# Tokens loaded in quarters of columns, the transposed banks read by ScalarE alone, squares after the tiles, two idle products

## What is computed

```python
h = rms_norm(x, norm1)
z = h @ w_in                        # 2048 x 5120: u, q, f, i, g
pool_out = pool_mix(u)              # trailing means over 2/4/8/16 tokens, a linear map for each group
o = hgrn2_recurrence(q, f, i) ...   # 8 heads, 128 x 128 state, norm and gate
x = x + concat(pool_out, o) @ w_o
x = x + (silu(h2 @ w_gate) * (h2 @ w_up)) @ w_down     # h2 = rms_norm(x, norm2)
y = rms_norm(x, norm_f)
```

## Time and profile before

| | us |
|---|---|
| median of the runs | 1494.37 |
| lowest, highest | 1490.41, 1495.2 |
| span of the profiled execution (first to last instruction) | 1492.4 |
| PE busy | 1459.7 (98%) |
| DVE busy | 805.1 (54%) |
| ACT busy | 550.0 (37%) |
| POOL busy | 188.2 (13%) |

### The profile page before, as it was taken

One profiled execution on the slowest core, in us unless ns is written; L12 is line 12 of the kernel. 1 busy time (PEld: TensorE's weight loads), 2 busy tenths in 40 slices (PEclk: granted clock), 3 DMA queues, 4 the chain that ended last, 5 costly groups with the idle time before them and its releaser, 6 DMA issues.

```text
span 1492.4 us, 27027 instructions
## 1 busy us (share of the span) xinstructions
PE 1459.7 (98%) x9928; PEld 1439.3 (96%) x9928; DVE 805.1 (54%) x1200; ACT 550.0 (37%) x823; POOL 188.2 (13%) x202
## 2 busy tenths in 40 slices
PE   7999999999999999999999999999999999999996
PEld 5999999899999999999999999999999999999996
DVE  4656788877765554444444544444444444444443
ACT  6442443344443343333333333333333333333443
POOL 0253434333112210000000000000000000000131
PEclk9998999999999999999999999999999999999998
DMA  8444544444465555554565555565554556555453
GB/s 223 137 129 124 138 122 137 119 114 122 124 168 141 148 145 157 141 156 123 150 185 144 142 141 142 140 168 150 159 141 133 149 147 165 154 152 141 119 148 114
DMA packets 409519, 214.52 MB, mean 144 GB/s; under 512 B 4093, under 2 KB 407757, under 8 KB 409420
## 3 DMA queue, kind: packets, MB, share of 16 engines
q1 hardware_dynamic: 391207, 203.52, 50.1%
q10 hardware_dynamic: 18277, 10.52, 2.6%
HBM read 206.14 MB, written 7.89 MB: 143 GB/s over the span
## 4 chain that ended last, share of the span: by engine, by line
PE 83%; DVE 10%; issue 4%; ACT 2%; DMA 1%; DVEq 0%; ACTq 0%; SPq 0%
PE bank L366 26%; PE bank L367 26%; PE bank L368 26%; DVE qr L1193 2%; DVE w_lo L1016 2%; DVE t L1180 1%; ACT w_hi L685 1%; DVE sc L1208 1%; PE bank L512 1%; DMA xt<-in_x_sample 1%; PE bank L462 0%; DVE sn L1252 0%; DVE scs L1208 0%; PE bank L410 0%; PE bank L412 0%
## 5 line engine op out<-in xcount | busy, mean ns | idle before, releaser
L366 PE MATMUL bank<-a_hi,w_hi 128*128 128x320 f32 x2048 | 646.2, 316 | 0.0
L367 PE MATMUL bank<-a_lo,w_hi 128*128 128x320 f32 x2048 | 635.4, 310 | 0.0
L368 PE MATMUL bank<-a_hi,w_lo 128*128 128x320 f32 x2048 | 635.3, 310 | 0.0
L1016 DVE TENSOR_TENSOR w_lo<-w_raw,w_hi 128x1024 fp32r<-128x1024 f32 (+1 forms) x416 | 467.3, 1164 | 150.1 <-ACT w_hi L685 149.2
L685 ACT ACTIVATE w_hi<-w_raw 128x1024 fp32r<-128x1024 f32 (+1 forms) x416 | 387.4, 968 | 158.5 <-PE bank L368 148.3
L366 PEld LDWEIGHTS bank<-a_hi,w_hi 128*128 128x128 f32 x2048 | 386.9, 189 | 2.4
L367 PEld LDWEIGHTS bank<-a_lo,w_hi 128*128 128x128 f32 x2048 | 387.2, 189 | 0.7
L368 PEld LDWEIGHTS bank<-a_hi,w_lo 128*128 128x128 f32 x2048 | 386.8, 189 | 0.0
L366 PE MATMUL bank<-h_hi,w_hi 128*128 128x320 f32 x704 | 217.7, 309 | 0.0
L367 PE MATMUL bank<-h_lo,w_hi 128*128 128x320 f32 x704 | 216.5, 308 | 0.0
L368 PE MATMUL bank<-h_hi,w_lo 128*128 128x320 f32 x704 | 216.5, 308 | 0.0
(11 more groups left out here) (218 smaller groups left out, 1195.6 us busy)
## 6 DMA issues: line engine op xcount, KB each, us to landing
w_raw<-in_w_gate SPq DMA_DIRECT2D x44, 1024.0 KB, 5.6
w_raw<-in_w_up SPq DMA_DIRECT2D x44, 1024.0 KB, 5.6
w_raw<-in_w_down SPq DMA_DIRECT2D x64, 704.0 KB, 4.8
w_raw<-in_w_in SPq DMA_DIRECT2D x39, 1024.0 KB, 5.8
w_raw<-in_w_o SPq DMA_DIRECT2D x16, 1024.0 KB, 6.1
s<-in_state_hgrn ACTq DMA_DIRECT2D x8, 512.0 KB, 4.3
out<-sn ACTq DMA_DIRECT2D x8, 512.0 KB, 7.3
xt<-in_x_prompt SPq DMA_DIRECT2D x3, 512.0 KB, 9.2
```

The lines of the kernel that those rows point to most:

```text
L366: pe.matmul(out, whi[:, par_, cols], r_hi, start=(k == 0), stop=False)
L367: pe.matmul(out, whi[:, par_, cols], r_lo, start=False, stop=False)
L368: last = pe.matmul(out, wlo[:, par_, cols], r_hi, start=False, stop=(k == last_k))
L1016: dve.tensor_tensor(wlo[:, par_, cols], raw[:, par_, cols], whi[:, par_, cols].bitcast(F32), SUB)\
```

## The change

Tokens are loaded in four quarters of 512 columns, not in two halves of 1024. SyncE's order becomes: first and second quarter of the first prompt tile and the samples, the first 8 tiles of slab 0, then third and fourth quarter of all three token tiles. ScalarE's queue issues two quarters of the second prompt tile. TensorE waits for a quarter ahead of tiles 0, 4, 8 and 12.

ScalarE copies every transposed tile to `x_res`, and takes a_hi from the bank for odd tiles alone. VectorE no longer reads the banks: for even tiles it takes a_hi from `x_res` (a tensor_scalar), and a_lo of all tiles from `x_res`. Four banks are free for reuse by one count, `xres_act`. ScalarE's two pieces of slab 0 follow tiles 3 and 11 (1 and 8 before), VectorE's follow tiles 4 and 12 (3 and 9 before). The lower bound's maximum stands after slab 1.

All six squares stand on ScalarE after slab 1. TensorE does two products of the matrix of ones by 512 columns of ones into a bank that is not in use yet, one ahead of the identity's wait and one behind norm1's transpose.

```diff
--- before.py
+++ after.py
@@ -28,6 +28,7 @@
 D = 2048
 KD = D // P
 HD = D // 2
+QD = D // 4
 TP, NB, TS = 256, 8, 8
 NS = NB * TS
 HB, HS = NB // 2, NS // 2
@@ -199,14 +200,14 @@
         ident_loaded, masks_loaded, norm1_loaded, par_loaded, w0_loaded, wp_loaded, cache_loaded, s0_loaded = (
             sem(n) for n in ("ident_loaded", "masks_loaded", "norm1_loaded", "par_loaded", "w0_loaded", "wp_loaded",
                              "cache_loaded", "s0_loaded"))
-        x_loaded = [[sem(f"x_loaded{half}{i}") for i in range(3)] for half in range(2)]
+        x_loaded = [[sem(f"x_loaded{quarter}{i}") for i in range(3)] for quarter in range(4)]
         fill_done, par_t, par_ready, lb_max, lb_exp, lb_ready = (
             sem(n) for n in ("fill_done", "par_t", "par_ready", "lb_max", "lb_exp", "lb_ready"))
         dve_link, newton_step = sem("dve_link"), sem("newton_step")
         ss_ready, rms_std, rms_diag, rms_bcast, rms_ready, stat_mm = (
             sem(n) for n in ("ss_ready", "rms_std", "rms_diag", "rms_bcast", "rms_ready", "stat_mm"))
-        xt_t, xres_act, ahi_ready, alo_ready = (
-            sem(n) for n in ("xt_t", "xres_act", "ahi_ready", "alo_ready"))
+        xt_t, xres_act, ahi_act, ahi_dve, alo_ready = (
+            sem(n) for n in ("xt_t", "xres_act", "ahi_act", "ahi_dve", "alo_ready"))
         t_ones, tails_ready, sc_zero, acc_zero, pad_zero, cache_tr, cache_in, win_step, win_ready, fix_ready, pooled_ready = (
             sem(n) for n in ("t_ones", "tails_ready", "sc_zero", "acc_zero", "pad_zero", "cache_tr", "cache_in", "win_step", "win_ready", "fix_ready",
                              "pooled_ready"))
@@ -281,11 +282,11 @@
                     eng.dma_start(prow[at:at + rows, :], src).then_inc(signal, 16)
                 at += rows
 
-        def load_x(eng, half, i):
-
-            cols = slice(half * HD, (half + 1) * HD)
+        def load_x(eng, quarter, i):
+
+            cols = slice(quarter * QD, (quarter + 1) * QD)
             rows, src = (P, x_prompt[0, i * P:(i + 1) * P, cols]) if i < 2 else (NS, x_sample.rearrange("b t d -> (b t) d")[:, cols])
-            eng.dma_start(xt[0:rows, i, cols], src).then_inc(x_loaded[half][i], 16)
+            eng.dma_start(xt[0:rows, i, cols], src).then_inc(x_loaded[quarter][i], 16)
 
 
         @block.sync
@@ -301,11 +302,14 @@
             sp.dma_start(cst[:, C_ID:C_ID + P], consts[:, C_ID:C_ID + P]).then_inc(ident_loaded, 16)
             load_x(sp, 0, 0)
             load_x(sp, 0, 2)
+            load_x(sp, 1, 0)
+            load_x(sp, 1, 2)
             w0 = raw[:, 0, :].rearrange("p (k c) -> p k c", c=P)
             k_mid = HALF[0][1]
             sp.dma_start(w0[:, 0:k_mid, :], win_v[:, 0:k_mid, 0:P]).then_inc(w0_loaded, 16)
-            for i in range(3):
-                load_x(sp, 1, i)
+            for quarter in range(2, 4):
+                for i in range(3):
+                    load_x(sp, quarter, i)
             sp.dma_start(w0[:, k_mid:KD, :], win_v[:, k_mid:KD, 0:P]).then_inc(raw_loaded[0], 16)
             load_params(sp, PARAMS[1:], par_loaded)
             load(1, 1, win_v, (0, KD), P)
@@ -401,20 +405,29 @@
 
             def x_transposes(k):
 
-                if k % (KD // 2) == 0:
+                if k % (KD // 4) == 0:
                     for i in range(3):
-                        pe.wait_ge(x_loaded[k // (KD // 2)][i], 16)
+                        pe.wait_ge(x_loaded[k // (KD // 4)][i], 16)
                 b4 = (SA, SB, SC, TV)[k % 4]
                 if k >= 4:
-                    pe.wait_ge((xres_act, alo_ready)[k % 2], (k // 2 - 1, k - 3)[k % 2])
+                    pe.wait_ge(xres_act, k - 3)
                 pe.transpose(b4[:, 0:P], xt[:, 0, k * P:(k + 1) * P], ident)
                 pe.transpose(b4[:, P:TP], xt[:, 1, k * P:(k + 1) * P], ident)
                 pe.transpose(b4[:, TP:N], xt[0:NS, 2, k * P:(k + 1) * P], ident[0:NS, 0:NS]).then_inc(xt_t, 1)
 
 
+            def keep_busy(count):
+
+                for _ in range(count):
+                    pe.matmul(zb[1][:, :].rearrange("p (a b) -> p a b", b=P), ones[:, :],
+                              ones[:, :].unsqueeze(1).to_broadcast([P, 4, P]), start=True, stop=True)
+
+            pe.wait_ge(fill_done, 1)
+            keep_busy(1)
             pe.wait_ge(ident_loaded, 16)
             pe.wait_ge(norm1_loaded, 16)
             pe.transpose(TK[:, 0:KD], prow[0:KD, :], ident[0:KD, 0:KD]).then_inc(par_t, 1)
+            keep_busy(1)
             for k in range(AHEAD):
                 x_transposes(k)
 
@@ -425,7 +438,7 @@
                 if k == 2:
                     pe.wait_ge(par_loaded, 16 * (len(PARAMS) - 1))
                     pe.transpose(TK[:, P:P + n_par], prow, ident[0:n_par, 0:n_par]).then_inc(par_t, 1)
-                pe.wait_ge(ahi_ready, k + 1)
+                pe.wait_ge((ahi_dve, ahi_act)[k % 2], k // 2 + 1)
                 pe.wait_ge(alo_ready, k + 1)
 
             def rms_first():
@@ -687,37 +700,36 @@
 
             load_params(act, PARAMS[:1], norm1_loaded)
             load_x(act, 0, 1)
+            load_x(act, 1, 1)
 
             act.wait_ge(fill_done, 3)
             act.activation(warm[:, 0:1], epst[:, 0:1], ACT.Sqrt)
 
             def square(half, i):
                 rows, at = (P if i < 2 else NS), 2 * i + half
-                act.wait_ge(x_loaded[half][i], 16)
+                for quarter in range(2 * half, 2 * half + 2):
+                    act.wait_ge(x_loaded[quarter][i], 16)
                 after(act, ss_ready, 3 * half + i)
                 act.activation(junk[0:rows, :], xt[0:rows, i, half * HD:(half + 1) * HD], ACT.Square,
                                accum_out=stat[0:rows, at:at + 1]).then_inc(ss_ready, 1)
 
-            for i in range(2):
-                square(0, i)
             act.wait_ge(par_ready, 1)
             for k in range(KD):
                 act.wait_ge(xt_t, k + 1)
                 bk = (SA, SB, SC, TV)[k % 4]
-                act.activation(a_hi[:, k, :], bk[:, 0:N], ACT.Copy, scale=pcol("norm1", k)).then_inc(ahi_ready, 1)
-                if k % 2 == 0:
-                    act.activation(x1[:, k, :], bk[:, 0:N], ACT.Copy).then_inc(xres_act, 1)
-                if k == 1:
+                if k % 2 == 1:
+                    act.activation(a_hi[:, k, :], bk[:, 0:N], ACT.Copy, scale=pcol("norm1", k)).then_inc(ahi_act, 1)
+                act.activation(x1[:, k, :], bk[:, 0:N], ACT.Copy).then_inc(xres_act, 1)
+                if k == 3:
                     act.wait_ge(w0_loaded, 16)
                     hi_piece(0, 0, 0, HALF[0])
-                if k == 3:
-                    square(0, 2)
-                if k == 8:
+                if k == 11:
                     act.wait_ge(raw_loaded[0], 16)
                     hi_piece(0, 0, 1, HALF[1])
             split_hi(1, 1)
-            for i in range(3):
-                square(1, i)
+            for half in range(2):
+                for i in range(3):
+                    square(half, i)
             act.wait_ge(ss_ready, 7)
             act.activation(stat[:, 9:12], stat[:, 6:9], ACT.Sqrt, bias=epst[:, 0:1], scale=1.0 / D).then_inc(rms_std, 1)
 
@@ -1055,23 +1067,29 @@
                 link(dve.tensor_tensor(lbt[:, 4, :], lbt[:, 1, :], lbt[:, 0, :], MUL))
                 dve.tensor_scalar(lbt[:, 5, :], lbt[:, 4, :], -1.0, 1.0, MUL, ADD).then_inc(lb_ready, 1)
 
-            for k in range(KD):
-                bk = (SA, SB, SC, TV)[k % 4]
-                dve.wait_ge(ahi_ready, k + 1)
-                if k % 2 == 1:
-                    dve.tensor_copy(x1[:, k, :], bk[:, 0:N])
-                else:
-                    dve.wait_ge(xres_act, k // 2 + 1)
-                src = (x1[:, k, :], bk[:, 0:N])[k % 2]
-                dve.scalar_tensor_tensor(out=a_lo[:, k, :], in0=src, scalar=pcol("norm1", k),
+            def normed_hi(k):
+
+                dve.wait_ge(xres_act, k + 1)
+                dve.tensor_scalar(a_hi[:, k, :], x1[:, k, :], pcol("norm1", k), None, MUL).then_inc(ahi_dve, 1)
+
+            def normed_lo(k):
+                dve.wait_ge(xres_act, k + 1)
+                dve.wait_ge((ahi_dve, ahi_act)[k % 2], k // 2 + 1)
+                dve.scalar_tensor_tensor(out=a_lo[:, k, :], in0=x1[:, k, :], scalar=pcol("norm1", k),
                                          in1=a_hi[:, k, :].bitcast(F32), op0=MUL, op1=SUB).then_inc(alo_ready, 1)
-                if k == 3:
+
+            for k in range(0, KD, 2):
+                normed_hi(k)
+                if k:
+                    normed_lo(k - 1)
+                normed_lo(k)
+                if k == 4:
                     lo_piece(0, 0, 0, HALF[0])
-                if k == 9:
+                if k == 12:
                     lo_piece(0, 0, 1, HALF[1])
-                if k == 12:
-                    lower_bound_max()
+            normed_lo(KD - 1)
             split_lo(1, 1)
+            lower_bound_max()
             dve.wait_ge(ss_ready, 6)
```

## The result

| | before | after |
|---|---|---|
| median, us | 1494.37 (17 runs, 1486.14 to 1495.44) | 1499.53 (17 runs, 1496.43 to 1500.95) |
| ratio of after to before | | 1.0039, 95% interval 1.0028 to 1.0050 |
| profiled execution, its own time (span) | 1494.37 (1492.4) | 1498.68 (1496.6) |
| first transpose of tokens, us | 9.66 | 8.31 |
| first product, us | 17.86 | 17.63 |

The medians are 5.2 us apart, and the ratio is 0.39% over 1. The forecast was 1495.4, 1.0 us slower, with a range up to 1498.2; it had the sign right and missed the size, and the measured time lies over the range.

The account below looks back on a forecast made before the run. TensorE, busy 98% of the span, was taken to set the time. Start -2.7, split's order +1.3 and squares +2.4 summed to +1.0 us: 1495.4 us, range 1488.4 to 1498.2.

Parts of the forecast that it names:

- Transposes start at 6.9: At the start, the samples' first quarter lands at 6.8 (bounds 6.2 to 7.6), so transposes start 2.7 us sooner.
- The new wait for `w_lo`: Ahead of the ninth tile's transposes, TensorE idles from 14.2 to 15.5; first product at 16.4, leaving 1.4 us gained.
- the landing L: Landing of the samples' first token quarter, taken as 6.8 us; the w_lo piece is ready at L + 8.7.
- The squares follow the tiles: First norm: six squares on ScalarE after slab 1 make TensorE wait 2.4 us, until 42.0, for the norm's products.
- No slack behind 42 us: After the first norm nothing is changed and PE has no slack, so the 1.0 us loss stays.
- The clock falls in the wait: In the new wait before the norm's products the clock falls; +1.8 us, up to +5; chance 0.12.
- rival (b): Slower: the clock falls in the new wait before the norm's products; 1497.2, up to 1500.4 us; chance 0.12.
- (c): At the start, quarters land no sooner than 8 us since the queues interleave; +1.2 more, 1496.6 us; chance 0.08.
- The idle products: Ahead of the tokens, two products on ones end by 4.9 us, cost nothing and bring no clock gain.
- Rival (a): The clock stays up from the idle products on; -6.0 us at the norm, 1488.4 or 1490.3; chance 0.18.

Follow-up runs that it names:

- the run with the wait filled: Changed kernel with three idle products of 512 columns ahead of TensorE's wait for the norm's diagonals; 1495.03 us, ratio 1.0015.
- the dense start on the changed kernel: Changed kernel with three squares back in the loop, five idle products ahead of the tokens, eight short ones among transposes, one long ahead of unit 0; 1484.65 us.
- the early pieces: Changed kernel with slab 0's first pieces sooner, w_hi behind tile 1 and w_lo behind tile 2; 1499.28 us, ratio 1.0034.
- the run with everything together: Changed kernel with first quarter alone in the queues, slab 0's first pieces sooner, three squares in the loop, five idle products and eight short ones; 1488.01 us.

## Why the prediction was wrong, by its own steps

**Transposes start at 6.9: missed by 1.4 us.** Measured 8.31. The landing that I put at 6.8, and at 7.6 if ScalarE's second quarter ran level, was at 8.17: that case was the true one, and it cost 0.6 us more than its bound. The run with the first quarter alone in the queues landed at 6.7, where I had put the value for the undisturbed queue (6.8). The mistake was to take the undisturbed case although the change itself put a second transfer into ScalarE's queue. The lag in bytes from one place can't be carried to another when what follows in the queues is different.

**The new wait for `w_lo`: right.** 1.3 us predicted, 1.09 measured; the first product stands 9.6 us behind the landing L in my sum (8.7 + 0.92), 9.5 in the trace. With the true L the sum gives 17.8, and 17.63 was measured. The gain at the first product, 1.4 us forecast, was 0.2.

**The squares follow the tiles: right in mechanism, and short by what the start had lost.** ScalarE's last tile came at 30.59 (29.4 forecast), the squares were 1.265 us apart (1.235), and the norm's products at 43.29 (42.0). Take the late start of 1.2 us off, and 0.1 us is left.

**No slack behind 42 us: right.** The 2.3 to 2.4 us are still there 80 us later, at the pause (127.41 against 125.04).

**The clock falls in the wait: this is the step that failed.** The sum priced the new wait by its length alone and put the clock behind it at nothing; it stood only as rival (b), with a chance of 0.12 and a price of 1.8 us. It fell in three profiled runs with late squares (at 45.1, 43.1 and 41.6 us), where it cost 1.7, 2.9 and 3.2 us, and in each of them delay and clock add up to the longer span within 0.2 us. My reason against it was wrong too: I said that the wait had to grow past the 2.4 us of the sum. A wait of 1.95 us was enough, and the row that I cited myself had a pause of 1.99 us, shorter than the wait that I forecast. In the changed kernel's own profiled run a wait of 1.76 us had no fall behind it. For its other runs the fall is inferred: from their mean clocks, and from the run with the wait filled, where it fits a gain of some 2 us.

With the clock in the sum: 1.0 + 1.3 for the late start + 1.8 for the clock = 4.1, and 1498.5 with the 1494.4 of before, against 1499.5 measured. Some 1 us is open; the price of 1.8 was at the low end of the 1.7 to 3.2 us seen, and the profiled run, without the fall, stayed low for 3.4 us longer at 127.5 to 141.2 us. I also kept (b) and (c) apart, as if only one could come. (c), a first quarter that lands after 8 us, came with the landing at 8.17, and the range ended below the sum of the two.

**The idle products: right that they bring nothing; the reason is only half borne out.** No gain, and no cost that could be told: the clock was lost at 8.1, before the first product. I had named the idle time and the transposes as what would lose it. In the profiled run it fell in the idle time, ahead of the first transpose of tokens, and in the run with five idle products it outlasted 4.6 us of transposes and fell in the wait behind them. The Trainium skill, "TensorE: Matmul & The Clock Gate", Part 4, says that transposes in PE mode do not count as busy for the clock in the way products do. The traces agree in so far as the transposes of the kernel before, at the lower level from 9.66 us, did not raise it; that transposes lose a raised clock no run here shows.

**Rival (a): near in its price, for another kernel.** In the dense start on the changed kernel, with the clock held, the loop takes 1.06 us a tile, not 0.92, and unit 2 starts 5.3 us sooner, where I had 6.0.

## What to carry to other kernels

Work taken out of an engine's idle time and put behind the loop has its own due time: ask when its result is needed, and count the engine's whole queue up to there. Price a new wait of TensorE twice, once for the delay and once for a stretch at half clock behind it; here waits of 1.95 to 4.26 us had such a stretch, and cost 1.7 to 3.2 us more than the delay. And before deepening any pipeline look at which clock the start runs at: here idle products that left TensorE no long wait in the start were worth 8 us, more than every rearrangement of the loads.

## What the runs showed of the hardware that I had not expected

- The granted-clock column reads 1.00 ahead of the first recorded rise or fall. In the kernel before the whole start to 34 us reads 1.00 and ran at 1.2 GHz; only the distance between products (0.27 against 0.15 us) tells.
- In the loop where transposes and products alternate, the clock stayed low in the traces of the two kernels, but it rose there in two others (at 28.0 us with the early pieces, at 23.3 us with the wait filled: 24 records in the stretch of 24 to 28 us, and 16 in the one before). So the loop is no safe sign of either level, and I had read it as one.
- Behind a pause of 2.0 us among small products, at 123 to 125 us, the clock was low for 10.2 us in the trace of the kernel before, 5.1 us of time, and by their mean clocks in most of its runs. With two idle products in the pause eight of twelve runs show no low stretch, and the profiled one held the clock there. The kernel before has runs as far apart as 1486.1 and 1495.4 us, and the fastest of them are those with the higher mean clock.
- Every fall of the clock on record in the first 150 us of these traces came in a wait of TensorE or up to 1.5 us behind one. These waits were 1.83 to 4.26 us long. Length alone doesn't sort them: in the run with everything together the pause of 1.96 us had no fall behind it.
- A DMA of 128 KB landed 1.5 us sooner when a 256 KB transfer behind it in another queue was moved to its own queue's end.
